# Turning the last twelve normed row tiles by transposing DMAs, with new planning estimates for such transfers

## The reference

```
h = h + W_out( sum_i sigmoid(gate_i(n)) * P_i(branch_i(n)) )
h = h + W2 relu(W1 RMSNorm(h))^2
```

## Time and profile before

| | |
|---|---|
| time, median of 3 runs | 2384.38 us (2383.14 to 2616.1) |
| time of the profiled execution | 2381.28 us |
| its span on the slowest core | 2380.2 us |
| spans of the eight cores | 2371.6 to 2380.2 us |
| TensorE busy | 2323.0 us, 98% of the span |
| VectorE, ScalarE, GpSimd busy | 54%, 37%, 10% |
| chain that ended last | TensorE 91%, VectorE 3%, issue 2%, ScalarE 2%, DMA 2% |
| turned by DMA | 22 tiles through hx (median 3.1 us to landing), 17 through fx (3.3 us) |
| 1 MB loads of feed-forward weights | 32 issues, median 13.1 us to landing |

### The profile page before, as it was taken

How to read it: one execution, slowest core, us unless ns; L and a number is a source line. 1 busy time by engine, 2 the same in 40 slices (tenths; PEclk the granted TensorE clock), 3 DMA queues, 4 the chain that set the end, 5 groups by cost and what they waited for, 6 DMA issues and landing times.

```text
span 2380.2 us, 40912 instructions; the slowest of 8 cores (2371.6 to 2380.2 us)
## 1 busy us (share of the span) xinstructions
PE 2323.0 (98%) x13392; PEld 1236.5 (52%) x13392; DVE 1273.8 (54%) x2231; ACT 886.3 (37%) x1810; POOL 245.9 (10%) x266
## 2 busy tenths in 40 slices
PE   6899999999999999999999999999999999999998
PEld 4576555546445454545455555564554454545453
DVE  3787776444465444434567776744434644434355
ACT  3877753222233121212456678322222421211133
POOL 2123222000000000000012233200000000000000
PEclk9999999999999999999999999999999999999999
DMA  9554936154186040406492467451815642222112
GB/s 162 143 165 122 186 125 142 71 97 111 70 159 103 1 72 1 76 1 116 127 164 74 149 137 157 100 135 63 142 72 107 126 65 36 36 37 36 18 59 93
DMA packets 219415, 229.41 MB, mean 96 GB/s; under 512 B 54315, under 2 KB 203307, under 8 KB 216106
## 3 DMA queue, kind: packets, MB, share of 16 engines
q0 software_dynamic: 83584, 78.45, 23.8%
q1 hardware_dynamic: 135626, 148.35, 20.9%
HBM read 240.41 MB, written 55.05 MB: 124 GB/s over the span
## 4 chain that ended last, share of the span: by engine, by line
PE 91%; DVE 3%; issue 2%; ACT 2%; DMA 2%; POOL 0%; DVEq 0%; ACTq 0%; SPq 0%; POOLq 0%
PE ps L454 90%; DMA wring<-w_in 1%; PE ps L467 1%; DVE U L428 0%; DMA Sf<-sgla 0%; DVE Sf L428 0%; ACT rsg L417 0%; DVE tmp L428 0%; ACT L417 0%; ACT tmp L417 0%; DVE sqg L425 0%; DVE lv L815 0%; ACT Sb L417 0%; DVE pt L425 0%; ACT xj L417 0%
## 5 line engine op out<-in xcount | busy, mean ns | idle before, releaser
L454 PE MATMUL ps<-hn,wring 128*128 128x384 bf16 (+1 forms) x6400 | 1245.4, 347 | 7.8 <-DVE sgt L425 1.7
L454 PEld LDWEIGHTS ps<-hn,wring 128*128 128x128 bf16 x6400 | 621.6, 98 | 545.4 <-issue 13.4
L454 PE MATMUL ps<-wring,a 128*128 128x512 bf16 x2176 | 476.0, 379 | 0.2 <-DVE a L425 0.2
L417 ACT ACTIVATE rl<-ps 128x384 f32<-128x384 f32 (+1 forms) x320 | 169.9, 532 | 637.9 <-PE ps L454 522.2
L425 DVE TENSOR_TENSOR h<-h,ps 128x512 f32<-128x512 f32 x340 | 233.1, 687 | 277.1 <-PE ps L454 276.1
L454 PEld LDWEIGHTS ps<-wring,a 128*128 128x128 bf16 x2176 | 212.8, 98 | 255.1 <-issue 0.7
L425 DVE TENSOR_TENSOR a<-rl 128x384 bf16<-128x384 f32 (+1 forms) x320 | 194.9, 612 | 276.0 <-ACT rl L417 268.0
L417 ACT ACTIVATE sg<-ps 128x384 f32<-128x384 f32 (+1 forms) x240 | 127.9, 533 | 450.3 <-PE ps L454 322.3
L454 PE MATMUL ps<-wring,hn 128*128 128x256 bf16 (+1 forms) x1088 | 193.7, 330 | 12.2 <-DMA wring<-w_in 10.8
L425 DVE TENSOR_TENSOR tmp<-sg,ps 128x384 f32<-128x384 f32 (+1 forms) x160 | 97.3, 608 | 154.4 <-ACT sg L417 79.1
L454 PEld LDWEIGHTS ps<-wring,hn 128*128 128x128 bf16 x1088 | 105.2, 99 | 79.3 <-issue 15.3
(11 more groups left out here) (137 smaller groups left out, 1777.6 us busy)
## 6 DMA issues: line engine op xcount, KB each, us to landing
wring<-w_ff POOLq DMA_DIRECT2D x32, 1024.0 KB, 13.1
wring<-w_in POOLq DMA_DIRECT2D x28, 1024.0 KB, 16.1
Sf<-sgla SPq DMA_DIRECT2D x64, 256.0 KB, 3.7
gla_s<-Sf SPq DMA_DIRECT2D x64, 256.0 KB, 2.8
H4s<-H_d SPq DMA_DIRECT2D x12, 768.0 KB, 8.5
OBs<-OB_d SPq DMA_DIRECT2D x12, 768.0 KB, 5.0
h_d<-h SPq DMA_DIRECT2D x17, 512.0 KB, 2.7
h<-h_d SPq DMA_DIRECT2D x17, 512.0 KB, 9.9
```

The costliest lines, as they stand in the source:

```text
L417: op(ACT, lambda: nc.scalar.activation(out=now(out), in_=now(in_), func=func, **kw), reads, writes, occ, 125.0, SETS.get(func))
L454: inst = nc.tensor.matmul(now(m[0]), m[1], m[2], start=m[3], stop=m[4], **kw)
```

## The change

`out_block` now turns all its tiles by DMA, where it did so for blocks 2 to 4 (tiles 6 to 16): tiles 0 to 5 are new, in both layers. With the 17 at the change of layer these are all 51 normed tiles after the first pass. And the planner's estimates for a transposing DMA change: it holds SP for 1250 ns instead of 500, its bytes are counted once instead of three times (at 290 bytes a ns), and it lands 1500 ns after that instead of 3500. Other transfers keep their numbers: the fixed time only moves from `lay_out` into the node.

```diff
--- before.py
+++ after.py
@@ -320,7 +320,7 @@
                 work = n.byts / (290.0 if e == 3 else 150.0 if dma_at[4] < 20000.0 else 245.0)
                 both = max(0.0, other - at0)
                 dma_at[e] = at0 + (both + work - both / 2 if work > both / 2 else work * 2)
-                fin = dma_at[e] + (3500.0 if e == 3 else 2500.0)
+                fin = dma_at[e] + n.lat
             for b in n.tiles:
                 i = id(b)
                 if kof[i] is None:
@@ -382,9 +382,8 @@
             n = 4 if in_.dtype == F32 else 2
             for s in in_.shape:
                 n *= s
-            if turn:
-                n *= 3
-            record(self.E, fn, reads, writes, 500.0 if self.E is SP else 900.0, 0.0, byts=n, after=after)
+            record(self.E, fn, reads, writes, 1250.0 if turn else 500.0 if self.E is SP else 900.0,
+                   1500.0 if turn else 3500.0 if self.E is SP else 2500.0, byts=n, after=after)
 
         def all_toks(self):
             return [(s, 16 * c) for s, c in zip(self.sems, self.cnt) if c > 0]
@@ -675,7 +674,7 @@
                 nc.gpsimd.dma_start(out=view, in_=src).then_inc(slot_sem[k], 16)
                 slot_cnt[k] += 1
             release((slot_sem[k], 16 * slot_cnt[k]), rs, ws)
-        record(POOL, fn, (), [b] + (first[2 * k:2 * k + 2] if n in (NSLOT, NSLOT + 1) else []), 900.0 * len(todo), 0.0, byts=byts)
+        record(POOL, fn, (), [b] + (first[2 * k:2 * k + 2] if n in (NSLOT, NSLOT + 1) else []), 900.0 * len(todo), 2500.0, byts=byts)
         views[order[n][0]] = [b] + vs
 
     def wget(l, nm):
@@ -1141,7 +1140,7 @@
                          [s], [ps], late=mgk[b])
                 add_half(t, hf, ps)
         for t in tiles(b):
-            norm_to_hn(t, hB[t].t[:, :], hH[t], hj, hx[t % 2], turn=b >= 2)
+            norm_to_hn(t, hB[t].t[:, :], hH[t], hj, hx[t % 2], turn=True)
 
     def ff1(l, s, n, b):
         T = TB[b]
```

## The result

The changed kernel takes 2401.3 us (median of 5 runs, 2399.4 to 2407.4) against 2384.7 (median of 4) for the kernel before on the same chip: ratio 1.008, 95% interval 1.0068 to 1.0093. That is within the 2% of the verdict, and above the range of the prediction. The profiled execution took 2399.36 us.

A forecast was written before the change was run, and what follows sets the result against it. TensorE was taken as the bound. The 5.4 us won, less stalls and change-of-layer loss, gave core 1 +8.5, span 2387.7, plus 1.1 to the profiled time 2388.8; the median was predicted at 2390 us, range 2378 to 2397.

The forecast's parts named there:

- 5.4 us: Both output projections: TensorE no longer turns twelve tiles at 0.45 us each, a gain of 2.7 us a layer.
- The place of the stall at the first second-product group: Feed-forward after each projection: TensorE waits there for late squares, one idle mark of 3 to 5 us a layer.
- That core 1 became the slowest: Whole span: core 1 at 2387.7 us, from stalls of 5.6 us a layer and 2.7 at the change of layer.
- the first rival: After the projection: tile 15's DMA lands before E + 11, nobody waits, the gain stays: 2379 us; chance 17%.
- I take nothing for it: Early projection: tiles 0 and 1 meet a weight load's tail; 12.4 us wait under 13.8 of PSUM bank cover, cost zero.
- E: The end of the projection on TensorE, from which the forecast counts times; 739.5 us on core 5 before.
- the second rival: Inside the projection: the staging pair chokes it through three slowed pairs, 10 us a layer, about 2410 us; chance 5%.
- So tile 15's transfer will meet them as tile 13's did.: End of projection: tile 15's transfer meets two weight loads, takes 13.4 us and lands at E + 15.7 on core 5.
- The sum: Whole span: core 5 -5.4 + 4.7 + 4.3 + 0.5 = +4.1; core 1 -5.4 + 11.2 + 2.7 = +8.5 us.
- 16.9 less 11.0: First second-product group: the stall is tile 15's landing, counted from E, less 11.0 us of cover.
- The account by the shared bytes: Feed-forward's start: rl_144 lies in hx_149's bytes, so its ReLU waits until tile 15's DMA has read them.
- The 0.5 and 2.7 us: Change of layer: VectorE's gate scans stand behind other work, costing 0.5 us on core 5 and 2.7 on core 1.

The follow-up runs named there:

- e6_plain_copy: The changed kernel with a plain DMA in place of each transposing one, same bytes and order; ratio 1.0085 to the kernel before.
- e2_est_only: The kernel before with the new transfer estimates alone, tiles 0 to 5 still turned by TensorE; ratio 1.0059 to the kernel before.
- e5_three_held: The changed kernel with three weight loads (a10, a11, b10) held until tile 16's transposing DMA has landed; ratio 0.9997 to the kernel before.
- e8_stage_moved: The changed kernel with the second staging buffer of tiles 7 to 15 moved out of rl_144's bytes, still two buffers; ratio 1.0086 to the kernel before.
- e7_filler: e2_est_only plus 20 unread matmuls on TensorE ahead of the first second-product group in each layer; ratio 1.0088 to the kernel before.
- e11_fx_only: The kernel before with the new estimates only for transfers through fx, at the change of layer; ratio 1.0013 to the kernel before.
- e3_ring_held: The changed kernel with the two weight loads a11 and b10 held until tile 16's transposing DMA has landed; ratio 0.9995 to the kernel before.
- e9_held_hx: e5_three_held with the new estimates only for the projections' transfers and the old ones at the change of layer; ratio 0.9978 to the kernel before.
- e4_three_stage: The changed kernel with three staging buffers for tiles 6 to 16, none in rl_144's bytes; ratio 1.0017 to the kernel before.

## Why the prediction was wrong

**Right.** TensorE was the bound. The twelve tiles gave 5.4 us: each projection is 2.7 us shorter (2.5 on one core) in every run with turn=True, where no mark stands inside it. The place of the stall at the first second-product group was as said, with a square that ends it and a ReLU that waits for tile 15's transfer ahead of that; on core 5 it stood there in both layers, on core 1 in layer 1 only. That core 1 became the slowest was said for another reason, and in three of the five executions it was another core. The Trainium skill's statement that transposing DMAs are as fast as regular ones ("Advanced Engine Details and Errata", section "X-Bar Transpose (TRN2)") agrees with e6_plain_copy, 3.0 against 2.9 us alone and, on core 0, 10.3 and 13.6 against 11.6 and 11.2 beside the loads; what does not follow from it is the first rival's early landing.

**The step that failed first: "I take nothing for it"**, said of tiles 0 and 1. The two transfers took 12.5 and 11.8 us on core 1, near the 13.4 that were allowed, and TensorE did not see it there, as argued. But cover at one place is not cover for what is handed on. VectorE lost 8.84 us, the norms behind ran later by a part of it, and at E tile 12's transfer met the new loads, with four norms still to come. The 10.8 us of core 1 (7.2 and 10.4 on cores 4 and 7) are the second rival's mechanism, the pair and the banks, at the other end of the projection; it had 5%. It is not the whole miss: core 3, with only 0.83 us of this wait, lost 13.8 us from the start of the projection on, and core 1 17.8. e2_est_only, without these transfers, has no such wait; e5_three_held, with them and without the load, has none either.

**The late square: "So tile 15's transfer will meet them as tile 13's did."** It did not. The sum had 4.7 and 4.3 us on core 5; measured were 5.83 and 5.31. But the transfers that met the loads were those of tiles 13 and 14 (10.8 and 13.9 us on core 5, layer 0). Tile 15's norm did not run 0.9 us after E: it shares its staging buffer with tile 13, and waited 6.99 us, to 743.86, until tile 13's transfer had landed. Tile 15 was issued at 745.2, took 5.3 us (3.0 to 9.0 on the eight cores, in either layer) where 13.4 were allowed, and landed at 750.5, E + 16.9, where E + 15.7 was predicted. It was issued 9.3 us later and took 8.1 us less than said; that the two nearly cancel in the landing is luck. The rest of the chain held: 16.9 less 11.0 is 5.9. The account by the shared bytes was not the only way: e8_stage_moved.

**A term that was missing: the clock behind a stall.** The sum counted idle time alone. The matmuls behind the idle marks took 2.3 to 2.8 us longer on cores 1 and 5. At the second product the late squares alone, at a granted clock of 1.00, are 0.7 of that (11.05 less 10.36, e7_filler), which leaves 1.6 to 2.1 to the half clock; at the first product of core 1, in layer 0, no square is waited for, and 15 of the 32 matmuls took 4.52 us at a granted clock of 0.50.

**Another: 1.0 us behind the last store.** From E in layer 1 to the end, all cores without a stall take 478.1 to 478.4 us where 39 later tiles are turned by DMA (the kernel before, e11_fx_only) and 479.1 to 479.5 where 51 are (e3_ring_held, e5_three_held, e9_held_hx). TensorE's pieces take the same time. The program ends with SP waiting, one after the other and always in the same order, for the 24 semaphores that its DMAs use in turn, and then for ten others. With 349 transfers on SP the last store has the thirteenth of the 24, and twelve waits are done while it is under way; with the 12 added ones, 361, it has the first, and all the others come behind its landing. The waits stand 0.05 us apart in the trace, so twelve are 0.6 us; the other 0.4 is a pause of 0.37 to 0.38 ahead of the seventh wait in every run with 361, whose cause is open. All eight cores of all 13 traces agree: 3.1 to 3.4 us from the issue of the last store to the end with 349, 4.1 to 4.5 with 361.

**The change of layer, mis-sized.** The 0.5 and 2.7 us were 0 in the profiled execution: on core 1 tile 16's norm waited 2.70 us, and TensorE has no idle mark there. But e11_fx_only and seven more have it, up to 8.8. The mechanism stood; one execution shows one draw of it.

With the terms as measured core 1 gives -5.4 + 10.8 + 2.6 + 5.9 + 2.8 + 1.0 = +17.7 where the sum had +8.5; the span grew by 19.1, of which 1.3 lie ahead of the projection.

## What to carry to other kernels

A planner's estimate for a transfer is a statement on what runs beside it: measure it beside the loads that the same event sets free, or hold those loads until the transfers have landed (some 13 us in e3_ring_held), which here was worth more than either estimate. When a wait is called covered, follow the waiting engine's queue to the end of the stage, not to the place where the cover ends, and give a stall of TensorE a second term for the clock behind it: 1.6 to 2.6 us behind the idle marks of 5 to 11 us here, none behind two of 2.1 and 2.4. What a transfer's length does should be read on all cores, since it differs by core and by execution.

## What had not been expected of the hardware

Beside a load of the weight ring it is not only the landing that is late. The second of two transposing DMAs kept SyncE for 7.7 us at its issue (core 1, 741.5) instead of 1.2, so whatever is queued behind it on SP waits as well: on core 0 of e4_three_stage an issue at 740.85 lasted 7.58 us, and the next transfer was issued at 748.57.

The cores come in pairs 0 and 1, 2 and 3, 4 and 5, 6 and 7. In the kernel before, one core of each pair begins the first projection 4 to 7 us after the other (676.7 and 672.3, 674.7 and 670.0, 678.1 and 671.4, 675.5 and 671.9), and the later ones are the slow ones. Which core is later changes from execution to execution: of the last pair it was 7 here and in the changed kernel, and 6 in e11_fx_only. The changed kernel's waits for a residual add are on exactly the four later cores (1, 3, 4 and 7), and so are the marks of layer 0 in e3_ring_held (0, 2, 5, 7) and in e4_three_stage (0, 2, 5, 6), and the stalls over 8 us in e8_stage_moved (0, 3, 4, 7). In the changed kernel tile 0's transfer took 10.2 to 12.5 us in layer 0 on the later cores and 8.4 to 10.0 on the others. Why a core is late, and why its transfers take longer, was not tried.
